# Triangle inversions of two chunks interleaved as four streams, sample state update between their steps

## The chip, the cores and the metric

One core of one Trainium2 chip runs the kernel in a single launch. The metric is device time in microseconds. The kernel before took 1852.71 us (median of three runs, 1852.44 to 1855.36).

## The reference

One inference step of a two-layer decoder with shared weights, for a prompt of 256 tokens and a sample batch of 8 sequences with one token each (264 token columns), all in float32. The first layer is a gated DeltaNet beside a cross-attention, the second a pooling mixer beside a cross-attention with eight experts behind it. The change lies in the DeltaNet alone:

```python
# prompt: chunked delta rule, 8 heads of 128x128
a_mat = I + where(strict, beta * (k k^T) * decay, 0)     # unit lower triangle
w_val, k_cd = solve(a_mat, [v * beta, k * beta * exp(G)])
for each chunk n:
    u = w_val - k_cd @ s
    o = (q * exp(G)) @ s + ((q k^T) * decay) @ u
    s = s * c_decay + k_tail^T @ u
# sample: one token for each of 8 sequences, 64 states of 128x128
s = s * exp(g);  u = b * (v - k @ s);  s = s + k^T u;  o = q @ s
# both: norm over each head, times silu(z), then the output projection
o = o * rsqrt(mean(o*o) + eps) * o_norm * silu(z)
h = x + concat([o, cross_attention]) @ w_out
```

## The kernel before

Everything is transposed: features lie on the 128 partitions, tokens along the free axis. The prompt's 256 tokens are two chunks (`NCH` = 2, the index `c`) of `P` = 128 tokens, with 8 heads (`H`), so that one array over all heads of a chunk is 128x1024 and fills one of the four two-bank PSUM tiles `PP[0..3]` (`bank(b)` is half of one). An ordinary float32 matmul appears as two passes in the trace (8 heads are x16), a transposition as one. Each engine runs its own list in the order in which it is written, and semaphores (`s("...")`) join the lists. There is no scheduler.

The part around the change has these steps:

- Preparation of a chunk. TensorE forms the broadcast cumulative gate (L1512, semaphore `dl_grow`), the two Gram products (L1516, `dl_kk`) and the broadcast beta (L1520, `dl_brow`). VectorE adds the mask (L997, `dl_neg`), ScalarE takes eight exponentials (L660) and one more (L662), VectorE forms `PTb` (L1002), `MTb` (L1004 and L1006), the decayed queries (L1009), the values by token (L1012) and `ktail` (L1014). TensorE transposes values and keys between them (L1527, L1531).
- Inversion of the unit triangle, in seven levels of block doubling (`NLVL` = 7). Level 0 is VectorE's alone (L1023, L1027). Each of the six others is a chain: VectorE masks `MTb` to `MLb` (L1023), TensorE transposes `Ub` (L1542), ScalarE copies it out (`Tb`, L668), TensorE multiplies (L1550), ScalarE copies (`Xb`, L671), TensorE multiplies (L1556), VectorE subtracts from `Ub` (L1032). The eight heads go in two groups of four. Chunk 1 starts when chunk 0 has been finished.
- The chunk's result: `solve` (L1570), copy (L673), output (L1578), state step (L1582), state (L1042, L1046, L1047). Chunk 1 needs the state of chunk 0 (L1564, L1037, L1038).
- The sample part, after both chunks: 64 products of keys and queries with the 64 states (L1593), a short chain on small tiles (L1079 to L1086), then four rounds `r` in which VectorE spreads the updates (`block`, L1093), TensorE forms outer products in four 32-row strips (`outer`, L1609), and VectorE updates 16 states (`new_state`, L360).
- The head norm over all 264 columns: squares (L690), sums (L1616), root (L692), gate (L1098), reciprocal (L1115), each head's row spread to all partitions (L1439), product (L1104). Then the halves for the output projection (L525, L844).
- The output projection `a_out`, 8 chunks of weights with 36 matmuls each (L1357). Large products work on float32r high and low halves: ScalarE forms the high half of the weights (`dense_high`, L334), VectorE the low half (`dense_low`, L340). Weights arrive in two raw slots `draw` at the start of `ring`; two sets of halves `dhi`, `dlo` follow, and their place holds the 64 sample states until these have been stored (POOL's queue, L463).

In the `order` rows below `gen`, `ring`, `ubuf` and `small` are the buffers out of which the arrays are cut; `PP` is PSUM.

## Time and profile before

| | us |
|---|---|
| median of three runs | 1852.71 |
| profiled execution, its own time | 1857.21 |
| its span | 1855.6 |
| PE busy | 1698.1 (92%) |
| DVE busy | 1291.1 (70%) |
| ACT busy | 1070.5 (58%) |
| DMA | 498.81 MB, mean 269 GB/s |

PE is TensorE's matmuls and PEld its weight loads, DVE is VectorE, ACT ScalarE, POOL GpSimd, SPq the DMA queue of SyncE. All times are us from the start of the span. A row of the timeline has the start, the duration from the first start to the last end, the engine, the line, the operation, tile written <- tiles read, the shape, the count, and in brackets the idle time before it and what ended that. A row of busy time by stretch has the stretch, its length, the busy time and count of PE, PEld, DVE, ACT and POOL, PE's granted clock as a share of 2.4 GHz, the share of the DMA engines and GB/s. A row of the chain of waits has start, duration, engine, tile, line and count. A row of DMA issues has the tile and source, the queue, count, size and median us from issue to landing.

### The profile page before, as it was taken

The page shows a single profiled execution, that of the slowest core. Times are in us where ns is not written, and L with a number is a line of the kernel's source. Part 1 is how long each engine was busy: PE and PEld are TensorE (multiplying, and loading weights), DVE is VectorE, ACT ScalarE, POOL GpSimd, SP SyncE. Part 2 cuts the span into 40 slices and gives each one's busy share as a digit, 9 for nine tenths or more (in the row PEclk, how much of TensorE's full clock was granted, in tenths as well). Part 3 has the DMA queues.
Part 4 walks back from the last instruction along what each step waited for, and adds up shares of the span by engine and source line. Part 5 has one row for each costly group of instructions (what it writes and reads, how often), then busy time and mean ns, then how long its engine had stood idle before and what let it go on. Part 6 is the DMA issues. An engine that isn't in the chain of part 4 may idle for free.

```text
span 1855.6 us, 25087 instructions
## 1 busy us (share of the span) xinstructions
PE 1698.1 (92%) x9859; PEld 1455.3 (78%) x9859; DVE 1291.1 (70%) x1160; ACT 1070.5 (58%) x1050; POOL 56.1 (3%) x80
## 2 busy tenths in 40 slices
PE   6999677878999986689999999999999999999993
PEld 6999466748999985587887878878878788787883
DVE  4596334375555455355888888888888888888886
ACT  5565223323443342244777777777777777777774
POOL 0000030000000000002000000000000000000001
PEclk9999779969999999687999999999999999999997
DMA  5555292025454542565999999999999999999993
GB/s 211 186 181 187 91 358 95 1 94 198 151 182 154 185 153 95 208 273 206 379 357 386 354 376 380 353 386 366 359 392 345 387 371 358 392 361 358 385 354 143
DMA packets 74675, 498.81 MB, mean 269 GB/s; under 512 B 8520, under 2 KB 8776, under 8 KB 20848
## 3 DMA queue, kind: packets, MB, share of 16 engines
q1 hardware_dynamic: 65680, 463.33, 65.7%
q0 software_dynamic: 8928, 34.54, 5.0%
q8 instruction: 48, 0.79, 0.2%
q14 instruction: 19, 0.16, 0.0%
HBM read 469.07 MB, written 28.77 MB: 268 GB/s over the span
## 4 chain that ended last, share of the span: by engine, by line
PE 84%; DVE 8%; ACT 4%; DMA 3%; issue 1%; POOL 0%; ACTq 0%; POOLq 0%; SPq 0%; DVEq 0%
PE PP L1357 71%; PE PP L1550 1%; ACT whi L769 1%; PE PP L1759 1%; PE PP L1556 1%; PE PP L1351 1%; DVE wlo L1218 1%; DMA ring<-in_kc 1%; PE PP L1735 1%; DVE ring L360 1%; DVE ring L1023 1%; DMA ring<-in_vc 1%; DVE dlo L340 1%; PE PP L1493 1%; PE PP L1467 0%
## 5 line engine op out<-in xcount | busy, mean ns | idle before, releaser
L1218 DVE TENSOR_TENSOR wlo<-raw,whi 128x2048 fp32r<-128x2048 f32 x339 | 775.1, 2291 | 139.4 <-ACT whi L769 139.1
L769 ACT ACTIVATE whi<-raw 128x2048 fp32r<-128x2048 f32 x339 | 649.3, 1919 | 229.9 <-PE PP L1357 229.8
L1357 PE MATMUL PP<-whi,xsh 128*128 128x512 f32 x896 | 359.3, 401 | 3.6 <-DVE xsl L1266 2.5
L1357 PE MATMUL PP<-wlo,xsh 128*128 128x512 f32 x896 | 354.9, 396 | 0.0
L1357 PE MATMUL PP<-whi,xsl 128*128 128x512 f32 x896 | 354.9, 396 | 0.0
L340 DVE TENSOR_TENSOR dlo<-ring,dhi 128x2048 fp32r<-128x2048 f32 (+2 forms) x86 | 177.9, 2069 | 144.6 <-ACT dhi L334 144.6
L334 ACT ACTIVATE dhi<-ring 128x2048 fp32r<-128x2048 f32 (+2 forms) x86 | 149.0, 1734 | 143.2 <-PE PP L1357 120.1
L1357 PE MATMUL PP<-uh,dhi 128*128 128x264 f32 x736 | 212.4, 289 | 8.9 <-DVE ul L844 8.4
L1357 PE MATMUL PP<-ul,dhi 128*128 128x264 f32 x736 | 210.9, 286 | 0.0
L1357 PE MATMUL PP<-uh,dlo 128*128 128x264 f32 x736 | 210.5, 286 | 0.0
L1357 PEld LDWEIGHTS PP<-whi,xsh 128*128 128x128 f32 x896 | 169.2, 189 | 46.5 <-DVE wlo L1218 5.4
L1357 PEld LDWEIGHTS PP<-whi,xsl 128*128 128x128 f32 x896 | 169.1, 189 | 40.6
L1357 PEld LDWEIGHTS PP<-wlo,xsh 128*128 128x128 f32 x896 | 169.3, 189 | 37.8
L1357 PE MATMUL PP<-whi,hTh 128*128 128x512 f32 x448 | 178.2, 398 | 0.0
L1357 PE MATMUL PP<-whi,hTl 128*128 128x512 f32 x448 | 176.9, 395 | 0.0
L1357 PE MATMUL PP<-wlo,hTh 128*128 128x512 f32 x448 | 176.9, 395 | 0.0
L1357 PEld LDWEIGHTS PP<-uh,dhi 128*128 128x128 f32 x736 | 140.4, 191 | 10.5 <-issue 9.1
L1357 PEld LDWEIGHTS PP<-ul,dhi 128*128 128x128 f32 x736 | 140.7, 191 | 0.0
L1357 PEld LDWEIGHTS PP<-uh,dlo 128*128 128x128 f32 x736 | 140.2, 191 | 0.0
L1357 PEld LDWEIGHTS PP<-whi,hTl 128*128 128x128 f32 x448 | 84.2, 188 | 20.0
L1357 PEld LDWEIGHTS PP<-wlo,hTh 128*128 128x128 f32 x448 | 84.3, 188 | 19.4
L1357 PEld LDWEIGHTS PP<-whi,hTh 128*128 128x128 f32 x448 | 84.3, 188 | 19.3
(374 smaller groups left out, 2011.6 us busy)
## 6 DMA issues: line engine op xcount, KB each, us to landing
raw<-in_w_e SPq DMA_DIRECT2D x339, 1024.0 KB, 4.9
ring<-in_wi SPq DMA_DIRECT2D x22, 1024.0 KB, 4.8
ring<-in_a_in SPq DMA_DIRECT2D x18, 1024.0 KB, 4.8
slot_rows<-ring POOLq DMA_DIRECT2D x25, 512.0 KB, 16.9
ring<-in_wo SPq DMA_DIRECT2D x16, 704.0 KB, 4.1
ring<-in_mkv SPq DMA_DIRECT2D x8, 1024.0 KB, 4.8
ring<-in_kc SPq DMA_DIRECT2D x8, 1024.0 KB, 6.1
ring<-in_vc SPq DMA_DIRECT2D x8, 1024.0 KB, 4.8
```

The lines of the kernel that those rows point to most:

```text
L334: a.activation(halves(n)[0], x, ACT.Copy).then_inc(s("d_hi"), 1)
L340: v.tensor_tensor(low, draw[n % DRAW][:, 0:WIDTH[DENSE[n][0]]], high.bitcast(F32), ALU.subtract)\
L360: ins_ = v.scalar_tensor_tensor(out=sl, in0=sl, scalar=sgb[:, n:n + 1], in1=bank(g)[:, q * P:(q + 1) * P], op0=ALU.mult, op1=ALU.add)
L769: a.activation(whi[c % XSET][:, :], raw_of(c), ACT.Copy).then_inc(s("w_hi"), 1)
L1023: v.tensor_tensor(heads(MLb), heads(MTb), mask, ALU.mult).then_inc(s("dl_ml"), 1)
L1218: v.tensor_tensor(wlo[c % XSET][:, :], raw_of(c), whi[c % XSET][:, :].bitcast(F32), ALU.subtract)\
L1351: mm = pe.matmul(bank(0)[:, 0:n], ones[:, :], sqb[:, k * n:(k + 1) * n], start=(k == 0), stop=(k == KD - 1))
L1357: mm = pe.matmul(out, lhs[l], rhs[r], start=first and i == 0, stop=last and i == 2)
L1493: mm = pe.matmul(bank(3)[32 * x:32 * x + 32, 0:P], p_diag[:, at_:at_ + 32], w[:, col:col + P], start=(b == 0 and m == 0), stop=(b == NS - ...
L1550: mm = pe.matmul(PP[1][:, x * P:(x + 1) * P], MLb[:, x * P:(x + 1) * P], Tb[:, x * P:(x + 1) * P], start=True, stop=True)
L1556: mm = pe.matmul(PP[2][:, x * P:(x + 1) * P], Xb[:, x * P:(x + 1) * P], Ub[:, x * P:(x + 1) * P], start=True, stop=True)
L1735: mm = pe.matmul(PP[1][:, k * C:(k + 1) * C], xtok[0:n, t, k * P:(k + 1) * P], disp[0:n, t, :], start=(t == 0), stop=(t == 2))
```

## The change

Both chunks are prepared first, chunk 1's products being issued between those of chunk 0. Their inversions run level by level together: four streams (`st`; chunk `st // 2`, heads `4 * (st % 2)` to `+ 3`), each in one PSUM bank (0 to 3) in which all three of its products land one after the other. The arrays of chunk 1 have places of their own: in `ubuf`, in the free end of `gen`, and in the two raw weight slots at the start of `ring`; therefore SyncE's loads of the first two `a_out` chunks wait for `dl_r` and for `dl_ds` 2. The sample part uses banks 4 to 7. Its columns are laid out right after the attention, its 64 products are issued ahead of level 1, its small chain stands in level 1, and its four rounds in levels 2 to 5. The head norm is made once for columns 0 to 127 and once for columns 128 to 263 (`parts`), the first while chunk 1's result is being formed. The halves of `cat` are formed in one instruction for attention, one for part 0 and two for part 1. POOL starts its 25 zero-fill DMAs at `state_loaded` and not at `dl_neg`, and stores the sample states before the prompt's state.

The diff, cut to what the prediction speaks of:

```diff
...
-        DTb, MTb, MLb, Xb, PTb, Sb = (cut(ring, arena + 1024 * i, 1024) for i in range(6))
+        DTb = cut(ring, arena, 1024)
+        MTb = [cut(ring, arena + 1024, 1024), cut(ring, 0, 1024)]
+        MLb = [cut(ring, arena + 2048, 1024), DTb]
+        PTb = [cut(ring, arena + 4096, 1024), cut(ring, 2048, 1024)]
...
-        Tb, Ub, vtok, ktail = (cut(gen, SC + 1024 * i, 1024) for i in range(4))
+        Tb = [cut(gen, SC, 1024), cut(ubuf, 1024, 1024)]
+        Ub = [cut(gen, SC + 1024, 1024), cut(ubuf, 0, 1024)]
+        vtok = [cut(gen, SC + 2048, 1024), cut(ring, 1024, 1024)]
+        ktail = [cut(gen, SC + 3072, 1024), cut(ring, 3072, 1024)]
+        Sb = cut(gen, SC + 5840, 1024)
+        Xb = [cut(ring, arena + 3072, 1024), cut(gen, SC + 6864, 1024)]
...
+                if (kind, i) == ("a_out", 0):
+                    sp.wait_ge(s("dl_r"), 1)
+                if (kind, i) == ("a_out", 1):
+                    sp.wait_ge(s("dl_ds"), 2)
...
-            pool.wait_ge(s("dl_neg"), 1)
+            pool.wait_ge(s("state_loaded"), 64)
...
+            for lv in range(1, NLVL):
+                for st in range(4):
+                    a.wait_ge(s("dl_tt"), 4 * (lv - 1) + st + 1)
+                    a.activation(half(Tb[st // 2], st % 2), bank(st), ACT.Copy).then_inc(s("dl_t"), 1)
+                for st in range(4):
+                    a.wait_ge(s("dl_xx"), 4 * (lv - 1) + st + 1)
+                    a.activation(half(Xb[st // 2], st % 2), bank(st), ACT.Copy).then_inc(s("dl_x"), 1)
...
+            inverted(0)
+            a.wait_ge(s("dl_um"), 4 * NLVL)
+            a.wait_ge(s("att_cat"), 2)
+            a.activation(cat_h[:, H:H + XH, :], cat[:, H:H + XH, :], ACT.Copy).then_inc(s("m_hi"), 1)
+            a.wait_ge(s("dl_o"), 1)
+            a.activation(cat[:, 0:H, parts[0]], PP[3][:, :].rearrange("p (m c) -> p m c", m=H), ACT.Copy).then_inc(s("dl_cat"), 1)
+            a.wait_ge(s("dl_cat"), 1)
+            squares(0)
+            head_root(0)
+            inverted(1)
+            a.wait_ge(s("on_done"), 1)
+            a.activation(cat_h[:, 0:H, parts[0]], cat[:, 0:H, parts[0]], ACT.Copy).then_inc(s("m_hi"), 1)
+            a.wait_ge(s("state_stored0"), 32)
+            dense_high(a, AT["a_out", 0])
+            a.wait_ge(s("dl_o"), 2)
+            a.activation(cat[:, 0:H, SEQ - P:SEQ], PP[2][:, :].rearrange("p (m c) -> p m c", m=H), ACT.Copy).then_inc(s("dl_cat"), 1)
             a.wait_ge(s("dl_cat"), NCH)
             a.wait_ge(s("sd_cat"), 1)
-            for x in range(H):
-                a.activation(sq[:, x * T:(x + 1) * T], cat[:, x, :], ACT.Square).then_inc(s("on_sq"), 1)
-            a.wait_ge(s("on_mm"), 1)
-            a.activation(rt[:, 0:T], bank(4)[:, 0:T], ACT.Sqrt, bias=epsc[:, 0:1], scale=1.0 / P).then_inc(s("head_rt"), 1)
-
-            a.wait_ge(s("att_cat"), 2)
-            high(cath[0], cat, T, range(H, H + XH), lambda k: None)
-            a.wait_ge(s("state_stored0"), 32)
-            dense_high(a, AT["a_out", 0])
-            high(cath[0], cat, T, range(H), lambda k: a.wait_ge(s("on_done"), k + 1))
+            squares(1)
+            head_root(1)
+            for i in range(2):
+                a.wait_ge(s("on_done"), 2 + i)
+                a.activation(cat_h[:, 4 * i:4 * i + 4, parts[1]], cat[:, 4 * i:4 * i + 4, parts[1]], ACT.Copy).then_inc(s("m_hi"), 1)
...
+                if c:
+                    v.wait_ge(s("dl_dt"), H)
+                    v.wait_ge(s("dl_mt"), 2)
+                    first_level(0)
...
+            for lv in range(1, NLVL):
+                if lv == 1:
+                    sample_rows()
+                if lv == 2:
+                    block(0)
+                if 2 <= lv < 5:
+                    block(lv - 1)
+                if 2 <= lv < 6:
+                    new_state(v, lv - 2)
+                if lv + 1 < NLVL:
+                    level_mask(lv + 1, 0)
+                for st in range(4):
+                    v.wait_ge(s("dl_du"), 4 * (lv - 1) + st + 1)
+                    u_half = Ub[st // 2][:, st % 2 * 512:(st % 2 + 1) * 512]
+                    v.tensor_tensor(u_half, u_half, bank(st), ALU.subtract).then_inc(s("dl_um"), 1)
+                if lv + 1 < NLVL:
+                    level_mask(lv + 1, 1)
...
+            v.wait_ge(s("dl_ds"), 1)
+            v.tensor_copy(Sb, PP[2][:, :]).then_inc(s("S_done"), 1)
+            cat_low(H, H + XH, slice(0, T))
+            v.wait_ge(s("dl_ks"), 1)
+            link(v.tensor_tensor(heads(Xb[1]), heads(PP[0][:, :]), per_head(1, cbeG), ALU.mult))
+            v.tensor_tensor(Xb[1], vtok[1], Xb[1], ALU.subtract).then_inc(s("dl_r"), 1)
+            gated(0)
+            head_inverse(0)
+            v.wait_ge(s("on_mm"), 2)
+            v.tensor_tensor(cat[:, 0:H, parts[0]], cat[:, 0:H, parts[0]], heads(PP[3][:, :]), ALU.mult).then_inc(s("on_done"), 1)
+            cat_low(0, H, parts[0])
             dense_low(v, AT["a_out", 0])
+            gated(1)
...
+            v.wait_ge(s("dl_ds"), NCH)
+            v.wait_ge(s("dl_o"), NCH)
+            link(v.tensor_tensor(heads(Sb), heads(Sb), per_head(1, ceGl), ALU.mult))
+            v.tensor_tensor(Sb, Sb, PP[0][:, :], ALU.add).then_inc(s("S_done"), 1)
+            dense_low(v, AT["a_out", 1])
...
+            def four(st):
+                return range(4 * (st % 2), 4 * (st % 2) + 4)
+
+            for lv in range(1, NLVL):
+                n0 = 4 * (lv - 1)
+                for st in range(4):
+                    c = st // 2
+                    if lv == 1:
+                        pe.wait_ge(s("dl_kt") if c == 0 else s("dl_mt"), 1 if c == 0 else 3)
+                    pe.wait_ge(s("dl_um"), 4 * (lv - 1) + st + 1)
+                    for x in four(st):
+                        mm = pe.transpose(PP[c][:, head(x)], Ub[c][:, head(x)], ident)
+                    mm.then_inc(s("dl_tt"), 1)
+                if lv == 1:
+                    pe.wait_ge(s("sd_row"), 1)
+                    pe.transpose(bank(7)[:, 0:P], kqrow, ident).then_inc(s("sd_mm"), 1)
+                if 2 <= lv < 6:
+                    outer(lv - 2)
+                for st in range(4):
+                    c = st // 2
+                    pe.wait_ge(s("dl_ml"), 2 * lv + c + 1)
+                    pe.wait_ge(s("dl_t"), n0 + st + 1)
+                    for x in four(st):
+                        mm = pe.matmul(PP[c][:, head(x)], MLb[c][:, head(x)], Tb[c][:, head(x)], start=True, stop=True)
+                    mm.then_inc(s("dl_xx"), 1)
+                if lv == 1:
+                    pe.wait_ge(s("sd_u"), 1)
+                    pe.wait_ge(s("sd_row"), 2)
+                    pe.transpose(bank(6)[:, 0:P], upad, ident).then_inc(s("sd_rows"), 1)
+                for st in range(4):
+                    c = st // 2
+                    pe.wait_ge(s("dl_x"), n0 + st + 1)
+                    for x in four(st):
+                        mm = pe.matmul(PP[c][:, head(x)], Xb[c][:, head(x)], Ub[c][:, head(x)], start=True, stop=True)
+                    mm.then_inc(s("dl_du"), 1)
...
+            solve(0, vtok[0])
+            pe.wait_ge(s("state_new"), 14)
+            state_step(0, PP[2])
+            pe.wait_ge(s("state_new"), 16)
+            result(0, PP[3])
+            pe.wait_ge(s("S_done"), 1)
             for x in range(H):
-                j, r = x % 4, x // 4
-                pe.wait_ge(s("on_sq"), x + 1)
-                mm = pe.matmul(bank(4)[32 * j:32 * j + 32, 0:T], pick[:, 31 - r:63 - r], sq[:, x * T:(x + 1) * T],
-                               start=(r == 0), stop=(r == H // 4 - 1))
+                mm = pe.matmul(PP[0][:, head(x)], act[:, 8 + x, cols(1)], Sb[:, head(x)], start=True, stop=True)
+            mm.then_inc(s("dl_ks"), 1)
+            pe.wait_ge(s("dl_cat"), 1)
+            head_sums(0, bank(6), 0, P)
+            pe.wait_ge(s("dl_r"), 1)
+            solve(1, Xb[1])
+            pe.wait_ge(s("head_inv"), 2)
+            for x in range(H):
+                col = 32 * (x % 4) + x // 4
+                mm = pe.matmul(PP[3][:, head(x)], ident[:, col:col + 1].to_broadcast([P, P]), rs[:, 0:P], start=True, stop=True)
             mm.then_inc(s("on_mm"), 1)
-            outer(1)
-            pe.wait_ge(s("head_inv"), 2)
-            for x in range(4):
-                row_to_all(bank(4 + x)[:, 0:T], rs, x).then_inc(s("on_mm"), 1)
-            outer(2)
-            for x in range(4, H):
-                pe.wait_ge(s("on_done"), x - 3)
-                row_to_all(bank(4 + x % 4)[:, 0:T], rs, x).then_inc(s("on_mm"), 1)
-            outer(3)
-            pe.wait_ge(s("state_new"), 16)
-            pe.wait_ge(s("on_done"), H)
+            pe.wait_ge(s("dl_qd"), 2)
+            result(1, PP[2])
+            state_step(1, PP[0])
+            head_sums(1, bank(2), P, T - P)
+            pe.wait_ge(s("head_inv"), 3)
+            pe.wait_ge(s("dl_cat"), 2)
+            pe.wait_ge(s("on_done"), 1)
...
```

TensorE's list at the end of chunk 0's inversion, before the change; L1542, L1550 and L1556 are the transposition and the two products of a level, L1570 to L1582 the chunk's result, L1512 to L1531 the preparation of chunk 1:

```order
L1542 MATMUL PP<-consts,gen 128x128 x8
L1550 MATMUL PP<-gen,ring 128x128 x8
L1556 MATMUL PP<-gen,ring 128x128 x8
L1570 MATMUL PP<-gen 128x128 x8
L1578 MATMUL PP<-ring,gen 128x128 x8
L1582 MATMUL PP<-gen 128x128 x8
L1512 MATMUL PP<-consts,small 128x128 x8
L1516 MATMUL PP<-ring 128x128 x16
L1520 MATMUL PP<-consts,small 128x128 x8
L1527 MATMUL PP<-consts,ring 128x128 x8
L1531 MATMUL PP<-consts,ring 128x128 x8
```

And one of the levels 2 to 5 with the change; `gen` holds `Ub` of chunk 0 and `ubuf` that of chunk 1, L1649 is the transposition, L1635 the sample's outer products, L1661 and L1671 the two products:

```order
L1649 MATMUL PP<-consts,gen 128x128 x8
L1649 MATMUL PP<-consts,ubuf 128x128 x8
L1635 MATMUL PP<-gen 128x512 x4
L1661 MATMUL PP<-gen,ring 128x128 x8
L1661 MATMUL PP<-ubuf,ring 128x128 x8
L1671 MATMUL PP<-gen,ring 128x128 x8
L1671 MATMUL PP<-ubuf,gen 128x128 x8
```

A level now holds both chunks and one round of outer products; results and preparations have left the place between the levels.

VectorE's list of the sample rounds and the head norm before the change; L1093 is `block`, L360 `new_state`, L1098, L1115 and L1104 the head norm:

```order
L1093 TENSOR_TENSOR gen<-gen 128x512 x2
L1098 SCALAR_TENSOR_TENSOR gen<-ring,gains,gen 128x264 x4
L360 SCALAR_TENSOR_TENSOR ring<-ring,small,PP 128x128 x16
L1093 TENSOR_TENSOR gen<-gen 128x512
L1098 SCALAR_TENSOR_TENSOR gen<-ring,gains,gen 128x264 x4
L1115 RECIPROCAL gen<-gen 128x264
L360 SCALAR_TENSOR_TENSOR ring<-ring,small,PP 128x128 x16
L1093 TENSOR_TENSOR gen<-gen 128x512
L1104 TENSOR_TENSOR gen<-gen,PP 128x264 x4
L360 SCALAR_TENSOR_TENSOR ring<-ring,small,PP 128x128 x32
```

And from the mask of chunk 0 in level 2 on with the change; L1066 is the mask, L1141 the subtraction of chunk 0 (`gen`) and of chunk 1 (`ubuf`), L1124 `block`, L368 `new_state`:

```order
L1066 TENSOR_TENSOR ring<-ring,consts 128x1024
L1141 TENSOR_TENSOR gen<-gen,PP 128x512 x2
L1141 TENSOR_TENSOR ubuf<-ubuf,PP 128x512 x2
L1066 TENSOR_TENSOR ring<-ring,consts 128x1024
L1124 TENSOR_TENSOR gen<-gen 128x512
L368 SCALAR_TENSOR_TENSOR ring<-ring,small,PP 128x128 x16
```

Each round of 16 state updates stands between two masks of the inversion.

SyncE's list with the change, where the loads of the output projection's weights follow those of the sample states:

```order
L389 DMA ring<-in_state 128x2048 [waits ain_mm]
L389 DMA ring<-in_state 128x2048 x3
L398 DMA ring<-in_a_out 128x1536 [waits cache_mm,dl_r]
L398 DMA ring<-in_a_out 128x1536 [waits cache_mm,dl_ds]
L398 DMA ring<-in_a_out 128x1536 [waits d_lo] x6
```

Before, the first two of the eight `in_a_out` loads waited for `cache_mm` alone.

## Rows read from the trace of the kernel before

**Rows 1.** The page's chain that ended last, share of the span by engine:

```profile
PE 84%; DVE 8%; ACT 4%; DMA 3%; issue 1%; POOL 0%; ACTq 0%; POOLq 0%; SPq 0%; DVEq 0%
```

**Rows 2.** Busy time by stretch: preparation, result, levels, result, sample, projection, experts:

```profile
243.40:260.70 17.30, 12.22 (x80) 11.78 (x81) 10.36 (x10) 3.35 (x9) 11.55 (x19) 0.80 1.01 404
299.00:322.60 23.60, 15.25 (x129) 14.46 (x129) 11.56 (x12) 5.40 (x11) 0.00 (x0) 0.97 0.00 1
322.60:360.70 38.10, 32.81 (x240) 29.63 (x240) 16.06 (x19) 14.33 (x24) 0.00 (x0) 0.93 0.00 1
360.70:380.30 19.60, 11.36 (x80) 10.73 (x80) 6.64 (x21) 2.05 (x2) 0.55 (x1) 0.88 0.03 13
380.30:418.20 37.90, 28.09 (x197) 15.82 (x198) 30.32 (x95) 10.60 (x26) 2.13 (x4) 0.55 0.28 116
418.20:456.00 37.80, 37.67 (x288) 37.48 (x288) 21.26 (x27) 14.21 (x15) 0.00 (x0) 0.93 0.54 185
850.00:1150.00 300.00, 298.67 (x1313) 241.35 (x1314) 255.34 (x157) 222.15 (x147) 11.80 (x12) 0.99 0.94 365
```

**Rows 3.** Timeline of one inversion level of chunk 0:

```profile
292.17 0.66 PE L1542 MATMUL PP<-consts,gen 128*128 128x128 f32 x4
292.86 0.60 ACT L668 ACTIVATE gen<-PP 128x512 f32<-128x512 f32 x1 [1.79 <-PE PP L1542]
...
293.11 1.23 DVE L1023 TENSOR_TENSOR ring<-ring,consts 128x1024 f32<-128x1024 f32 x1
...
294.39 2.05 PE L1550 MATMUL PP<-gen,ring 128*128 128x128 f32 x16 [0.67 <-DVE ring L1023]
...
296.28 2.01 PE L1556 MATMUL PP<-gen,ring 128*128 128x128 f32 x16
...
297.43 0.69 DVE L1032 TENSOR_TENSOR gen<-gen,PP 128x512 f32<-128x512 f32 x1 [3.10 <-PE PP L1556]
298.33 0.69 DVE L1032 TENSOR_TENSOR gen<-gen,PP 128x512 f32<-128x512 f32 x1 [0.21 <-PE PP L1556]
```

**Rows 4.** Timeline, the first level of chunk 1:

```profile
324.41 3.73 PE L1550 MATMUL PP<-gen,ring 128*128 128x128 f32 x16
```

**Rows 5.** Timeline of chunk 1's preparation:

```profile
309.34 3.74 PE L1516 MATMUL PP<-ring 128*128 128x128 f32 x32
...
310.87 2.44 ACT L660 ACTIVATE ring<-ring,small 128x128 f32<-128x128 f32 x8 [5.52 <-DVE ring L997]
...
313.22 1.00 ACT L662 ACTIVATE ring<-PP 128x1024 f32<-128x1024 f32 x1
...
316.99 1.23 DVE L1009 TENSOR_TENSOR ring<-ring 128x1024 f32<-128x1024 f32 x1
318.14 1.22 DVE L1012 TENSOR_TENSOR gen<-PP,small 128x1024 f32<-128x1024 f32 x1
```

**Rows 6.** Timeline of the sample part:

```profile
380.36 6.42 PE L1593 MATMUL PP<-ring,gen 128*32 128x128 f32 x128 [4.52 <-DVE gen L1074]
...
390.21 2.09 PE L1609 MATMUL PP<-gen 32*128 32x512 f32 x8 [1.19 <-DVE gen L1093]
...
392.29 4.22 DVE L360 SCALAR_TENSOR_TENSOR ring<-ring,small,PP 128x128 f32<-128x128 f32 x16
...
398.65 1.80 DVE L1115 RECIPROCAL gen<-gen 128x264 f32<-128x264 f32 x1
```

**Rows 7.** Timeline, the halves of the first output-projection weights:

```profile
408.94 1.48 ACT L334 ACTIVATE dhi<-ring 128x1536 fp32r<-128x1536 f32 x1 [12.93 <-DMA out_state<-ring]
...
415.98 1.75 DVE L340 TENSOR_TENSOR dlo<-ring,dhi 128x1536 fp32r<-128x1536 f32 x1
```

**Rows 8.** Chain of waits, the output projection:

```profile
418.23 37.68 PE PP L1357 x288
```

**Rows 9.** DMA issues of the output projection's weights and the prompt's state:

```profile
ring<-in_a_out SPq DMA_DIRECT2D x8, 768.0 KB, 4.3
...
out_S<-ring POOLq DMA_DIRECT2D x1, 512.0 KB, 2.9
```

More of the change, by code:

```diff
@@ L227, in build @@
         kqrow = cut(gen, DS + 704, 128)
-        kpad = cut(gen, DS + 1728, 128)
-        upad = cut(gen, DS + 1856, 128)
-        own16 = cut(gen, DS + 1984, 16)
-        assert 4096 + 2000 <= SCN
+        own16 = cut(gen, DS + 1728, 16)
+        kpad, upad = (cut(ring, arena + 6400 + 128 * i, 128) for i in range(2))
+        assert 4096 + 1744 <= 5840 and 6400 + 256 <= CT * PRE
         urow = cut(gen, DS + 576, 128)
@@ new lines, in inverted, with squares @@
+            def inverted(c):
+                for g in range(2):
+                    a.wait_ge(s("dl_uu"), 2 * c + g + 1)
+                    a.activation(half(Tb[c], g), bank(2 * c + g), ACT.Copy).then_inc(s("dl_u"), 1)
+            cat_h = cath[0].rearrange("p (k t) -> p k t", t=T)
+            parts = (slice(0, P), slice(P, T))
+            def squares(c):
+                sqv = sq.rearrange("p (k t) -> p k t", t=T)
+                a.activation(sqv[:, :, parts[c]], cat[:, 0:H, parts[c]], ACT.Square).then_inc(s("on_sq"), 1)
@@ L1124, in _ @@
-            dense_low(v, AT["a_out", 0])
-            v.wait_ge(s("S_stored"), 16)
-            for k in range(H, H + XH):
-                low(catl[0], cath[0], cat, T, k)
-            for k in range(H):
-                low(catl[0], cath[0], cat, T, k)
-            dense_low(v, AT["a_out", 1])
-            def residual(name, chunks):
+            for lv in range(1, NLVL):
[15 more added lines that the diff above has]
+                    level_mask(lv + 1, 1)
@@ L1581, in _ @@
-                for x in range(H):
-                    mm = pe.matmul(PP[3][:, x * P:(x + 1) * P], ktail[:, x * P:(x + 1) * P], uu[:, x * P:(x + 1) * P],
-                                   start=True, stop=True)
-                mm.then_inc(s("dl_ds"), 1)
-            pe.wait_ge(s("dl_cat"), NCH)
-            pe.wait_ge(s("S_done"), NCH)
+            pe.wait_ge(s("att_cat"), 2)
+            grow(0, PP[0])
+            gram(0, 0, PP[1])
+            gram(0, 8, PP[2])
+            brow(0, PP[3])
@@ new lines, in solve, with state_step @@
+            def solve(c, R):
+                for g in range(2):
+                    pe.wait_ge(s("dl_um"), 4 * (NLVL - 1) + 2 * c + g + 1)
+                    for x in four(g):
+                        mm = pe.matmul(PP[c][:, head(x)], Ub[c][:, head(x)], R[:, head(x)], start=True, stop=True)
+                    mm.then_inc(s("dl_uu"), 1)
+            def state_step(c, out):
+                for x in range(H):
+                    if x % 4 == 0:
+                        pe.wait_ge(s("dl_u"), 2 * c + x // 4 + 1)
+                    mm = pe.matmul(out[:, head(x)], ktail[c][:, head(x)], Tb[c][:, head(x)], start=True, stop=True)
+                mm.then_inc(s("dl_ds"), 1)
@@ L1632, in _ @@
+            pe.wait_ge(s("dl_cat"), 2)
+            pe.wait_ge(s("on_done"), 1)
+            for x in range(H):
+                at_, r = 32 * (x % 4), x // 4
+                mm = pe.matmul(bank(4 + x % 4)[:, r * (T - P):(r + 1) * (T - P)],
+                               ident[at_:at_ + 32, at_ + r:at_ + r + 1].to_broadcast([32, P]),
+                               rs[at_:at_ + 32, P:T], start=True, stop=True)
+            mm.then_inc(s("on_mm"), 1)
             order = [(k, k) for k in (*range(H, H + XH), *range(H))]
```

366 lines of the change are left out of this document (168 added, 198 removed).

## The prediction

> **What bounds the kernel now.** I read the page's chain of waits first: 84% of it is TensorE [rows 1], so only what shortens TensorE's path, or a stretch in which it waits, can show. Then busy time by stretch [rows 2]. The projection and the experts keep TensorE busy to over 99%, and the change does not touch them. Between the end of the attention (243.4) and the projection (418.2) that is not so: TensorE is busy for 12.2 of 17.3 us in the first preparation, 15.3 of 23.6 between the chunks, 11.4 of 19.6 behind chunk 1, and in the sample part for 28.1 of 37.9, there at a granted clock of 0.55, with VectorE busy for 30.3. Even the levels hold it for only 32.8 of 38.1 us. Third, the timeline of one level [rows 3] shows why: mask (1.23), product, product, subtraction run one behind the other. From the mask's start at 293.11, through the second product at 296.28, to the last subtraction at 298.33 plus 0.69, it is 5.9 us, 6.0 with the handover, in which TensorE has 40 passes. Twelve such levels are 72 us.
>
> **The change, on the time axis of the profile before.** Nothing moves before 243.4. The sample's column layout (2 us of small VectorE work) now stands there, beside TensorE's first products, and costs nothing: it used to follow chunk 1. Its cover is the 3.9 us between 243.4 and the first mask; without it, it would cost its 2 us.
>
> *Preparation of both chunks.* VectorE sets it. An operation of 128x1024 takes 1.23 us, and 1.15 from start to start where nothing is awaited (316.99 to 318.14) [rows 5]. Chunk 0 ends at about 258.4, as before. Chunk 1: gate mask 1.15 (259.6); the eight exponentials 2.44 on ScalarE (262.1), beside which VectorE makes level 0 of chunk 0; a ninth of 1.00 and TensorE's broadcast of beta, 16 passes at half of the 3.74 for 32, take until 265.1 [rows 5]; then the last product and three more, 1.23 + 3 x 1.15 = 4.7, to 269.8. Then TensorE makes the sample's 64 products, 6.42 [rows 6], and three small ones, 0.5: level 1 begins at 276.8. Beside them VectorE makes level 0 of chunk 1 and two masks, 1.2 + 1.3 + 2.3 = 4.8 us, which is covered.
>
> *Levels.* Both chunks make 80 passes in a level. 16 take 1.89 from start to start (294.39 to 296.28) [rows 3], so a level is 9.45 us if TensorE never waits. It need not: one stream's way through a level is 0.66 + 0.60 + 1.1 + 0.60 + 1.1 + 0.69 = 4.8 us, half a level, so three other streams cover it. ScalarE has eight copies of 0.60, 4.8 us. VectorE has two masks and four subtractions, 2 x 1.23 + 4 x 0.69 = 5.2 us. In levels 2 to 5 it also has 16 state updates, 4.22 [rows 6], and a `block` of the subtraction's shape, 0.69: 10.1 us. Outer products join TensorE there. Before, eight of their passes took 2.09 at half clock [rows 6]; at full clock they lie between half of that and all of it. I take 1.9, near the row, and keep 1.05 as the other end. So levels 2 to 5 are 11.35 on TensorE against 10.1 on VectorE, and TensorE leads. Level 1 has two small transpositions (0.4), level 2 waits for the first `block` (0.75). Sum: 9.85 + 12.1 + 3 x 11.35 + 9.45 = 65.45, from 276.8 to 342.2. Where VectorE leads instead, the four levels are 10.4 with handovers, so cheap outer products save at most 3.8.
>
> The Trainium skill (TensorEngine Tiling (Array Packing), Key Properties) speaks against this placing: a change of the tiling mode drains TensorE. Outer products of 32 rows now stand four times between full-array products, eight changes. The drain in this trace is what a run outlasts the start of the next: 2.05 against 1.89, 0.16 us [rows 3]. Eight of them are 1.3 us; by the rule the sum would be 1.3 later, inside my range; I leave it out, since nothing here shows a change of mode apart.
>
> *Behind the levels.* Chunk 0's solve, state step, output, and the keys times state are four runs of 16 passes, 7.6 (349.8, 350.0 with the tail). VectorE's two operations on the right side, 2 x 1.23, to 352.5. Solve of chunk 1, 1.9, to 354.4; at the same time VectorE's gate (1.25) and reciprocal (1.80 for 264 columns [rows 6], so 0.9 for 128), to 354.65. Spreading 1.9 (356.55), output of chunk 1 3.8 (360.3), state step 1.9 behind it (362.2). ScalarE has finished high halves of `cat` and weights by then (359.0 + 1.48 = 360.5 [rows 7]), copies the output (1.0), squares it (1.05): 362.6. Sums 0.8 (16 of the 128 passes in 6.42), root 0.4, reciprocal 0.95, spreading 1.1, two products 1.4, high and low half 0.65 each: 368.9. TensorE has meanwhile made the projection's attention part, begins with the heads at 368.9 and has 24 passes at 37.68 / 288 = 0.131 [rows 8], to 372.05. That rate contains an opening at half clock, as before. Then the second set of weights: VectorE makes its low half behind both halves of `cat` (369.6) and the state update (2 x 1.23), 1.75 [rows 7], ready at 373.85. Seven tiles of 36 passes, 33.0: end at 406.9.
>
> *DMAs.* The first two weight loads lose their early start. The first goes out at 352.5 and takes 4.3 [rows 9], 356.8, before ScalarE asks for it at 359.0: covered by 2.2 us. The second goes out at 362.3 and is there at 366.6, ScalarE comes to it at 368.8: covered by 2.2. The sample's stores end inside the levels (the last update is made near 328), and the 12.93 us that ScalarE waited for them go [rows 7]. The prompt's state is stored from 372.1 and takes 2.9 [rows 9]; VectorE waits for that (375.0) before the first residual addition and the third low half, which it then has at 377.2, while TensorE wants it at 378.6.
>
> *Sum.* Before, the stretch from 243.4 to the projection's end at 455.9 is 212.5 us; after it is 163.5. That is 49 us less. The profiled execution took 1857.2 (span 1855.6), so its like would take 1808; the median of the runs is 4.5 us below it, 1852.7, and the forecast for the median is 1804. What is late next is VectorE and ScalarE in turns between 350 and 374. All of the experts' stage is relative to what precedes it and moves along.
>
> **Rivals.**
>
> *Half clock behind the levels.* After its pause before 324.4, TensorE took 3.73 for 16 passes instead of 2.05 [rows 4, 3], and the sample part with its short runs had a clock of 0.55 [rows 2]. The new tail has pauses of 1 to 3 us too (350.0 to 352.5, 363.4 to 365, 366.1 to 368.9). If the clock falls at the first, solve, spreading, output and two small runs double: 1.9 + 1.9 + 3.8 + 1.4 = 9 us, giving 1813. For it: the pauses. Against: runs of 4 to 8 us stand between them. The Trainium skill (TensorE: Matmul & The Clock Gate, HAM oscillation) says that waits between bursts put the engine back to the half clock each time; if so here, it is this rival's time, and the sample part's 0.55 agrees.
>
> *VectorE becomes the bound of levels 2 to 5.* If its 4.22 + 0.69 of sample work does not fit beside the products, because it is queued between two masks and TensorE waits for the subtractions behind it, each of the four levels grows by up to 4.9 us: 19.6, giving 1824. For it: 10.1 of 11.35 us is little room. Against: the state updates wait only for outer products that stand early in the level, and the subtractions come last anyway.
>
> *Half clock in all levels, and slower than before.* The place is the six joint levels. If the mixture of 32-row and full-array passes with waits on four streams keeps the clock low, as in the sample part [rows 2], 80 passes take 18.9 instead of 9.45, 57 us more in all, giving 1861, 8 slower than now. It decides from 49 / 9.45 = 5.2 levels at half clock on. Against it: with pauses in every level, the chunk-1 stretch of before had a mean of 0.93, low only at its opening, and at 99% busy the experts have 0.99 [rows 2].
>
> *Better than the sum.* Outer products at 1.05, the sample's products faster at full clock than their 6.42, part of the weights' rate at full clock: 8 us, 1796.
>
> *The change doesn't do what it says.* The order shows that it does; waits which tie streams to each other would make a level as long as before, 12 us for both chunks, 15 us more, 1819.
>
> **Chances.** The sum, within 1799 to 1809: 0.58. Half clock behind the levels 0.17, better than the sum 0.10, VectorE as the bound 0.05, tied streams 0.03, the slower rival 0.03, and 0.04 for what I don't see. The range runs from 1793 (below the better case by its unknowns) to 1817 (above the half-clock case), leaving out 0.15 or so. About 0.2%, 3.7 us, is what a measurement of this kernel tells from no change: faster by more 0.95, within it 0.02, slower by more 0.03.
>
> **What would show it.** Right: levels 1 and 6 of 9.5 to 10 us and levels 2 to 5 of 10.4 to 11.5, TensorE over 95% busy there at a clock near 1; the first transposition of level 1 near 276.8; no wait of ScalarE for the state's stores; the projection's last matmul near 407. Wrong: subtractions that start more than 1 us behind their products (VectorE), passes of 0.23 us behind 350 (clock), TensorE waiting for halves of weights at the second or third tile (the delayed loads).

## Result and profile after

The changed kernel takes 1798.84 us (median of four runs), the kernel before 1852.62 beside it: a ratio of 0.9706, 95% interval 0.9682 to 0.9730. The forecast was 1804, with a range of 1793 to 1817. The four runs lie at 1795.7, 1796.2, 1801.5 and 1801.8; the profiled execution took 1801.81.

The head of the page of after, its TensorE line, the granted clock in 40 slices, and its chain by engine:

```profile
span 1800.2 us, 25098 instructions
...
PE 1674.6 (93%) x9891; PEld 1444.9 (80%) x9891; DVE 1287.6 (72%) x1142; ACT 1067.9 (59%) x1039; POOL 57.1 (3%) x81
...
PEclk9999869999999995969999999999999999999997
...
PE 86%; DVE 5%; ACT 4%; DMA 3%; issue 1%; POOL 0%; ACTq 0%; POOLq 0%; SPq 0%; DVEq 0%
```

Against 1698.1 us before, TensorE is busy for 23.5 us less, while its instructions are nearly the same. Part of that is clock: from the attention's end to the projection's, the granted clock was 0.85 before and is 0.95 now. Another part is not: a short run is counted as busy until its last pass has ended, so that the 40 passes of one of the old levels were busy for 5.1 us at a clock of 1.00, while 40 passes of a joint level take 4.45. The rest of the gain is idle time that went. Busy time by stretch of after (columns as in [rows 2]): preparation of both chunks with the sample's products, the six levels, the tail up to the projection's first heads, the projection, the experts.

```profile
243.30:275.20 31.90, 26.93 (x292) 26.10 (x292) 24.35 (x37) 6.96 (x19) 18.47 (x25) 0.85 0.87 296
275.20:334.80 59.60, 58.83 (x518) 55.05 (x517) 47.66 (x109) 27.20 (x51) 2.15 (x4) 1.00 0.49 175
334.80:362.60 27.80, 23.38 (x205) 21.97 (x203) 16.34 (x16) 13.37 (x17) 0.00 (x0) 0.88 0.24 86
362.60:398.70 36.10, 34.12 (x276) 33.69 (x276) 20.36 (x19) 14.21 (x15) 1.49 (x2) 1.00 0.52 182
850.00:1150.00 300.00, 299.66 (x1336) 242.10 (x1335) 259.29 (x143) 223.97 (x147) 2.17 (x4) 1.00 0.98 368
```

Where TensorE was busy for 32.8 of 38.1 us of one chunk's levels [rows 2], it is busy for 58.8 of 59.6 in those of both, at a clock of 1.00. The projection ends at 398.2 (its last pass begins at 397.95) where it ended at 455.9: 57.7 us of the stage are gone, and 49 were forecast. The experts have not changed.

The chain of waits of after through one joint level (start, duration, engine, tile, line, passes). L1649 are the transpositions, L1635 the outer products, L1661 and L1671 the two products:

```profile
295.47 1.75 PE PP L1649 x16
297.22 1.07 PE PP L1635 x8
298.29 3.77 PE PP L1661 x32
302.06 3.57 PE PP L1671 x32
305.63 1.75 PE PP L1649 x16
```

It holds TensorE alone: 10.16 us for both chunks, against 6.0 for one [rows 3]. The last level, without outer products, takes 8.9 (325.95 to 334.84).

### The profile page after: what moved, and what is told of

It reads as the page before. It is cut to its first block, busy times and chain, and to the rows that moved or that the text cites. A ratio compares the mean times of both kernels' runs of the same rounds, so it can differ in the third digit from the quotient of the medians.

```text
span 1800.2 us, 25098 instructions
## 1 busy us (share of the span) xinstructions
PE 1674.6 (93%) x9891; PEld 1444.9 (80%) x9891; DVE 1287.6 (72%) x1142; ACT 1067.9 (59%) x1039; POOL 57.1 (3%) x81
## 4 chain that ended last, share of the span: by engine, by line
PE 86%; DVE 5%; ACT 4%; DMA 3%; issue 1%; POOL 0%; ACTq 0%; POOLq 0%; SPq 0%; DVEq 0%
PE PP L1418 73%; ACT whi L809 1%; PE PP L1870 1%; PE PP L1661 1%; PE PP L1412 1%; PE PP L1671 1%; DMA ring<-in_vc 1%; DVE wlo L1279 1%; DMA ring<-in_kc 1%; PE PP L1846 1%; DVE dlo L348 1%; PE PP L1528 1%; ACT dhi L342 1%; PE PP L1554 1%; ACT L809 0%
```

## Experiments

The time is not the best measure of an edit here, since runs of one kernel differ by up to 7 us. The profile has a better one: the start of the sums of squares behind the projection (L1412; L1351 before), where the stage is over. From there to the end of the span is 1399.2 us before (from 456.42), 1401.1 after (from 399.12), and between 1397.9 and 1401.4 in all twelve other profiles. So each edit is read from the "end of the stage", and its median is set beside it. That measure has noise of its own, ahead of the levels: in the kernels whose preparation is the same, level 1 starts between 271.45 and 277.67, in part because TensorE's short runs there come at full or at half clock (the sample's 64 products took 3.70 in some profiles, 5.37 in others). Where an edit stands behind that point, the distance from there to the end of the stage says more.

### The changed kernel again

> The changed kernel again, for a closer ratio and a second profile: its four runs lay in two pairs, 1795.7 and 1796.2 against 1801.5 and 1801.8. Theory: the pairs come from where the half clock falls, so the mean granted clock goes with the time (0.955 against 0.950), and the stretch from 243 to the projection's end is the same within 1 us in both profiles. Rival: the joint levels themselves vary from run to run.

Five runs: median 1796.03 (1794.63 to 1799.07), ratio 0.9689 (0.9676 to 0.9703). In the nine runs so far the mean granted clock goes with the time, as expected: 0.950 to 0.953 in the three above 1799 us, 0.955 to 0.957 in the other six. The joint levels take 59.6 again. The stage ends at 398.72, 0.4 earlier; the span is 3.1 shorter. The chains of after and then of this profile show where most of it arises, in the next layer's attention:

```profile
674.72 5.97 PE PP L1528 x16
...
692.14 4.94 DMA ring<-in_vc
699.12 7.12 DMA ring<-in_vc
```

```profile
673.47 3.73 PE PP L1528 x16
...
695.54 6.46 DMA ring<-in_vc
```

The same 16 passes took 5.97 at a granted clock of 0.62 and 3.73 at one of 1.00 (2.2 us), and one wait for a cached V more in the chain. No edit here touches these; they set what two single runs can tell.

### Sample rounds behind the levels, then chunk by chunk, then the mask last

Three kernels, each built on the one before it. The first takes the outer products and state updates out of the levels and puts them between the last level and chunk 0's solve:

```diff
-                if 2 <= lv < 6:
-                    outer(lv - 2)
...
+            for r in range(4):
+                outer(r)
             solve(0, vtok[0])
```

> The changed kernel with the sample's four rounds (block, outer products, state updates) behind the six joint levels and ahead of chunk 0's solve. In the changed kernel the levels run from 275.2 to 334.8, 59.6 us. Theory (TensorE leads every level, the rounds ride beside it): the levels shrink only by their outer products (4 x 1.07) and the wait of level 2 (0.8), to 54.5 us, and the rounds, bare, cost VectorE's 4 x 4.2 + 1.3 = 18 us, of which TensorE waits about 15: 10 us slower than the changed kernel, about 1809, at 0.976 of before. Rival (VectorE leads the levels with a round, so a round costs nearly its own length there too): the levels shrink by 15 or more, and the time stays within 3 us of the changed kernel.

The second makes all levels of chunk 0 and then all of chunk 1, with two streams each; masks still stand ahead of the subtractions:

```diff
-            for lv in range(1, NLVL):
-                for st in range(4):
+            for k in range(2 * (NLVL - 1)):
+                c, lv = k // (NLVL - 1), k % (NLVL - 1) + 1
+                for g in range(2):
```

> As e1, and the levels chunk by chunk: two streams at a time, all six levels of chunk 0, then those of chunk 1, with the mask of the next level still formed ahead of the subtractions. Theory (only four streams keep TensorE busy; with two it waits for the copies and subtractions as in the kernel before): a level is about 6.0 us, 72 in all, 17 us slower than e1. Rival (what made the levels short is that the mask left the chain between subtraction and product): a stream's way is 4.8 us and TensorE's work for two streams 4.5, so a level is 5.0 to 5.3 us, 60 to 64 in all, 6 to 9 us slower than e1.

The third puts each mask behind the subtractions, as the kernel before had it:

```diff
-                if lv + 1 < NLVL:
-                    level_mask(lv + 1, c)
                 for g in range(2):
...
+                if lv + 1 < NLVL:
+                    v.wait_ge(s("dl_um"), 4 + 2 * k + 2)
+                    level_mask(lv + 1, c)
```

> As e2, with the mask of the next level behind the subtractions and awaited by the product, as in the kernel before. Both theories: 6.0 us a level, 72 in all, 17 us slower than e1; by the theory of the four streams no slower than e2, by the rival of the mask 8 to 12 us slower than e2. If it is well under 72, then the place of the mask is not what sets the 6.0 us of the kernel before.

| kernel | median | ratio, interval | levels (first start) | end of the stage |
|---|---|---|---|---|
| changed | 1798.84 | 0.9706 (0.9682 to 0.9730) | 59.6 (275.20) | 399.12 |
| rounds behind | 1811.19 | 0.9780 (0.9763 to 0.9796) | 53.8 (274.62) | 411.66 |
| by chunk | 1821.40 | 0.9836 (0.9820 to 0.9852) | 64.1 (273.80) | 421.06 |
| mask last | 1828.20 | 0.9874 (0.9857 to 0.9890) | 69.7 (271.45) | 426.65 |

Windows of the first kernel, its levels and then its rounds:

```profile
274.60:328.40 53.80, 53.76 (x484) 53.57 (x482) 29.81 (x41) 27.21 (x51) 0.00 (x0) 1.00 0.34 113
329.00:346.70 17.70, 15.67 (x33) 5.92 (x33) 17.09 (x62) 0.00 (x0) 1.62 (x3) 0.64 0.33 138
```

Without the rounds a level is 8.9 us of nothing but TensorE. Behind the levels they are VectorE's (17.1 of 17.7 us busy), and TensorE's clock falls to 0.64. From the last product of the levels to chunk 0's solve it is 18.3 us (328.4 to 346.7). So the rounds cost 18.3 alone and 5.8 inside: 12.5 us. That is the theory of the expectation, with 2.5 us more than it put down; the rival, in which VectorE leads the levels, is out.

The chain of the second kernel through a level of one chunk:

```profile
311.03 0.70 DVE ubuf L1137
311.78 0.66 PE PP L1648 x4
312.50 2.02 PE PP L1657 x16
314.52 1.86 PE PP L1666 x16
316.40 0.70 DVE ubuf L1137
```

5.37 us for 40 passes, which alone would be 4.45: the last subtraction and the handovers now stand in the chain. Two streams are not enough to cover what follows a product; four are. The levels are 10.3 us longer for it (64.1 against 53.8). Of the two expectations, the theory (6.0 us a level, 72 in all) was wrong, and the rival (5.0 to 5.3, 60 to 64) nearly right. In the third kernel the mask joins the chain:

```profile
312.26 1.24 DVE ring L1067
313.54 2.05 PE PP L1658 x16
315.59 1.86 PE PP L1667 x16
317.47 0.70 DVE ubuf L1135
318.19 1.24 DVE ring L1067
```

5.93 us, nearly the 6.0 of [rows 3]; the mask's place is worth 5.7 us of the levels (69.7 against 64.1), less than the 8 to 12 of the expectation. The stage ends 5.6 later too, but that is chance: level 1 began 2.35 earlier here, and behind the levels as much was lost again, most of it with chunk 1's solve, 3.64 at half clock against 2.05. So what the prediction put down as one thing, a TensorE that never waits, has two causes, the streams and the masks' place. The three steps make 27.5 of the 57.3 us, to within the 2 or 3 us by which the clock shifts such stages; the other 29.8 lie in what is common to all of them: one preparation for both chunks, the sample's small operations moved out of the way, the tail. They were not separated further, but for the next edit.

### Head norm behind chunk 1

The changed kernel with both halves of the norm behind chunk 1's output:

```diff
-            a.wait_ge(s("dl_cat"), 1)
-            squares(0)
-            head_root(0)
             inverted(1)
...
+            squares(0)
             squares(1)
+            head_root(0)
             head_root(1)
```

> The changed kernel with the whole head norm behind chunk 1's output, both column parts one right behind the other. Theory (part 0 of the norm is hidden beside chunk 1's solve and output): squares 1.1, sums 0.7, gate 1.3, reciprocal 0.95, spreading 1.8, product 1.2 and the halves 2.3 of part 0 come onto the path behind 354, some of it beside part 1: 5 to 8 us slower than the changed kernel. Rival (the path there is TensorE's own passes and the weights' halves, and the norm has room): under 2 us.

1808.92 (1805.09 to 1810.51), ratio 0.9763 (0.9747 to 0.9779). The stage ends at 407.40, 8.3 later; 1.3 of that arose ahead of the levels, so 7 are left for the norm's two parts; in them is a spreading of 16 passes at half clock, 3.34 (the changed kernel has 1.95 for its own). The expectation was 5 to 8; the medians are 10 to 13 apart, more than the stage explains.

### Does VectorE or TensorE set levels 2 to 5?

Three kernels, with one run each: a quarter of the state updates (three quarters of the sample's new state are left out), one more VectorE operation of 128x512 in each of levels 2 to 5, and the outer products made twice:

```diff
-                for q in range(4):
+                for q in range(1):
```

> The changed kernel with only 4 of the 16 state updates of each round, which leaves three quarters of the sample's new state out: VectorE is relieved of 3.1 us in each of levels 2 to 5. In the changed kernel such a level takes 10.16 us. Theory (TensorE leads): 10.1 to 10.2 again. Rival (VectorE leads, TensorE's work fits in less): down to 9.9 or less.

```diff
                     new_state(v, lv - 2)
+                    block(lv - 2, extra=True)
```

> The changed kernel with one more 128x512 operation of VectorE (0.65 us) in each of levels 2 to 5. VectorE's work there is 4.2 + 0.65 + 2 x 1.15 + 4 x 0.65 = 9.75 of 10.16 us. Theory (TensorE leads, but by 0.4 us only): the level grows by 0.2 to 0.4 us, to 10.4 to 10.6. Rival (ample room): 10.16. Rival (VectorE leads already): 10.8.

```diff
+                    pe.matmul(bank(4 + g), krow[32 * g:32 * g + 32, :], ublk[r % 2][32 * g:32 * g + 32, :], start=True, stop=True)
+                for g in range(4):
```

> The changed kernel with each round's outer products formed twice: TensorE has 8 more passes of 32 rows, about 1.07 us, in levels 2 to 5. Theory (TensorE leads): each level grows by 0.9 to 1.1 us. Rival (VectorE leads): by under 0.7.

The six levels, 59.6 in the changed kernel, take 59.6 with a quarter of the updates (277.67 to 337.32), 59.6 with more VectorE work (274.97 to 334.61) and 63.1 with twice the outer products (275.34 to 338.42). Times: 1802.79, 1801.60, 1803.64. TensorE sets the levels. I had expected a little growth from the added VectorE operation; there is none, so at least its 0.69 us fits into each level.

TensorE around the outer products, from the timeline of the kernel that makes them twice:

```profile
308.20 1.04 PE L1651 MATMUL PP<-consts,ubuf 128*128 128x128 f32 x8
...
309.17 1.14 PE L1635 MATMUL PP<-gen 32*128 32x512 f32 x8
...
310.13 1.04 PE L1637 MATMUL PP<-gen 32*128 32x512 f32 x8
...
311.10 2.05 PE L1663 MATMUL PP<-gen,ring 128*128 128x128 f32 x16
```

Eight more passes with no change of tiling cost 0.86 us a level (11.02 against 10.16), 0.108 each. The first eight cost 1.26 (10.16 against 8.90). The 0.40 between them goes with the two changes between full-array and 32-row passes: four times 0.40 is 1.6 us. The Trainium skill (TensorEngine Tiling (Array Packing), Key Properties) says that a change of mode drains the engine; the prediction put that at 1.3 by the tail of a run and left it out. The 1.6 agree with the rule, though a drain is not seen apart from whatever else happens at those borders.

### Three edits where the changed kernel still waits, and all together

Four rows of the chain of after stand for four places where it could be shorter:

```profile
262.82 3.67 PE PP L1582 x16
...
271.18 3.70 PE PP L1621 x128
...
344.69 3.68 PE PP L1679 x16
...
365.59 1.68 DVE dlo L348
```

beta's broadcast of chunk 1 at half clock, with VectorE waiting; the sample's 64 products ahead of level 1; chunk 1's solve at half clock; the low half of the second weights, made behind the state update. First, that low half goes ahead of the update:

```diff
+            dense_low(v, AT["a_out", 1])
             v.wait_ge(s("dl_ds"), NCH)
...
-            dense_low(v, AT["a_out", 1])
-            v.wait_ge(s("S_stored"), 16)
```

> The changed kernel with VectorE's low half of the second projection weights ahead of the update of the prompt's state, and the wait for that state's store moved from before the first residual addition to before the pooling input is written. In the changed kernel TensorE waits 1.50 us for this half at its second tile (365.8 to 367.3). Theory (the order on VectorE is what holds it): the wait goes to 0.1 or less, the projection ends 1.2 to 1.5 us earlier. Rival (the late load of the second weights holds it): the wait stays over 1 us.

Second, in the preparation, beta's broadcast waits for less (another PSUM tile), chunk 0's first mask and transpositions go ahead of the sample's:

```diff
-            pe.wait_ge(s("dl_neg"), 2)
-            pe.wait_ge(s("dl_eg"), 2)
-            brow(1, PP[2])
+            pe.wait_ge(s("dl_kt"), 1)
+            brow(1, PP[0])
```

> The changed kernel with chunk 1's broadcast of beta in the PSUM tile of chunk 0's keys, so that it need not wait for the ninth exponential, and the sample's 64 products in a bank of their own, ahead of chunk 1's last VectorE operations. In the changed kernel VectorE waits 2.35 us for the broadcast (formed at half clock, 3.65 us, after a pause of TensorE of 2.2), and the 64 products stand 4.0 us ahead of level 1. Theory (these two waits set the preparation): the first product of level 1 starts at 273 and not at 277.05, and the time falls by 3.5 to 4.5 us. Rival (VectorE's list alone sets it): it falls by 2.4 at most.

Third, matmuls without use fill two of TensorE's pauses in the tail:

```diff
+            for x in range(6):
+                pe.matmul(bank(3)[:, 0:P], ident, tri, start=True, stop=True)
             pe.wait_ge(s("dl_r"), 1)
             solve(1, Xb[1])
```

> The changed kernel with 12 and 14 idle passes of TensorE into a free bank in its two pauses behind the levels (343.2 to 344.7 and 356.7 to 358.4). In the changed kernel chunk 1's solve runs at half clock, 3.68 us instead of 1.9, and so do the first ten projection passes. Theory (the pauses bring the half clock, and short work in them prevents it): the solve takes 1.9, the passes 0.12 each, and the time falls by 2 to 3 us. Rival (the clock fell for what went before, the sum over it being low anyway): the solve still takes over 3 us, no gain.

Last, all three:

> The three edits of e8, e9 and e10 together. Theory (they stand in different places of one chain): the gains add, 7 to 9 us below the changed kernel, about 1788, at 0.965 of before. Rival (each moves the wait to another engine): 3 to 5 us.

| kernel | median (runs) | ratio, interval | end of the stage | from level 1's first product to there |
|---|---|---|---|---|
| changed | 1798.84 (1795.72 to 1801.81) | 0.9706 (0.9682 to 0.9730) | 399.12 | 122.1 |
| changed, again | 1796.03 (1794.63 to 1799.07) | 0.9689 (0.9676 to 0.9703) | 398.72 | 121.5 |
| low half first | 1798.46 (1796.39 to 1799.05) | 0.9693 (0.9672 to 0.9713) | 396.15 | 118.8 |
| preparation | 1795.43 (1793.78 to 1799.35) | 0.9684 (0.9661 to 0.9706) | 393.56 | 120.3 |
| filled pauses | 1797.87 (1797.02 to 1799.18) | 0.9692 (0.9672 to 0.9712) | 397.61 | 119.9 |
| all three | 1791.01 (1789.15 to 1796.14) | 0.9664 (0.9643 to 0.9685) | 389.81 | 118.2 |

Alone, none can be told from the changed kernel by its time. By the end of the stage they are 2.6 to 3.0, 5.2 to 5.6 and 1.1 to 1.5 us ahead, but not all of that is the edit. In all of them chunk 1's solve took 2.05 and not 3.68 or 3.49, and the first two edits touch nothing between the levels and that solve. Its row in the changed kernel and in that with the low half first:

```profile
344.69 3.68 PE L1679 MATMUL PP<-gen,ubuf 128*128 128x128 f32 x16 [1.42 <-DVE gen L1168]
```

```profile
344.99 2.05 PE L1679 MATMUL PP<-gen,ubuf 128*128 128x128 f32 x16 [1.43 <-DVE gen L1168]
```

What is left of each edit:

- Low half first: from the first pass with heads to the end of the stage it is 35.0 (from 361.14), against 36.1 to 36.5 in seven profiles in which TensorE waits 1.5 for that half. So its place is worth 1.1 to 1.5 us, as expected; the rest is the solve.
- Preparation: from chunk 1's exponentials to the first product of level 1 it is 14.1 us here and with all three edits, against 17.6 to 19.0 in the other kernels with joint levels. The first product starts at 273.27; 273 was expected. The rest, again, is the solve.
- Filled pauses: the 1.5 to 2.1 us behind level 1's first product are hardly more than what the preparation kernel has there without any filling (1.2 to 1.8).

Together the three are 8.9 to 9.3 ahead, near the sum and at the upper end of the 7 to 9 expected, with the lowest time of all: 5 us below the better of the two medians of the changed kernel. Of this, 1.7 us arose ahead of the three edits: chunk 1's exponentials began at 257.56, against 259.31 in the changed kernel. (The intervals of the ratios still touch, so 5 us is what the medians say, and 9 what the profiles say.) The chain of that version, the projection in one piece:

```profile
354.61 0.73 DVE catl L1160
355.39 33.91 PE PP L1418 x276
```

and its tail, at full clock where after had 0.88:

```profile
329.40:355.40 26.00, 23.62 (x231) 22.02 (x230) 16.37 (x16) 13.39 (x17) 0.00 (x0) 1.00 0.25 92
```

What the filling itself gives isn't settled, since chunk 1's solve ran at full clock in four kernels without it (rounds behind, by chunk, low half first, preparation). That in its own kernel no pass of the tail was slow (granted clock 1.00) is what was seen.

## Why the prediction was right

The mechanism is the one forecast, and the time, 1798.84 and then 1796.03, lies in the range. It lies just below the 1799 to 1809 of "the sum", though: the stage lost 57.7 us and not 49, and the terms below say where.

*What bounds it, and what leads in the levels: right.* TensorE leads; shown by adding and taking away VectorE work (nothing) and TensorE work (all of it). The rival with VectorE as the bound is out, as are tied streams and half clock in the levels (1.00 throughout).

*Preparation: right in its end, by two errors that cancel.* The first transposition of level 1 starts at 275.20, forecast 276.8. The timeline of after:

```profile
262.82 3.65 PE L1582 MATMUL PP<-consts,small 128*128 128x128 f32 x16 [2.22 <-ACT gen L678]
...
266.51 1.22 DVE L1092 TENSOR_TENSOR ring<-ring,PP 128x1024 f32<-128x1024 f32 x1 [2.35 <-PE PP L1582]
...
271.18 3.70 PE L1621 MATMUL PP<-ring,gen 128*32 128x128 f32 x128 [2.31 <-DVE ring L1098]
```

Beta's broadcast took 3.65 for the 1.9 of the sum: half clock, behind a pause of 2.22. The sample's products took 3.70 for 6.42: that row [rows 6] was itself at half clock, which its stretch's clock of 0.55 said [rows 2]. I named this as an error to come only in the rival "better than the sum". That the two cancel is luck, and so is the size of each: in the second profile of the changed kernel the broadcast took 2.50 and the products 5.37, and level 1 still started at 275.39.

*Levels: mis-sized.* 65.45 forecast, 59.6 measured. 80 passes take 8.9, not 9.45: I took 16 passes as 1.89 from start to start, which held 0.1 us of something that the interleaved streams don't show; 32 passes take 3.57, so 16 take 1.79. That is 3.3 over six levels. The outer products I took at 1.9, near a row at half clock, with 1.05 as the other end; eight of them take 1.07 in the chain and 1.26 with what they do to their neighbours: 2.6 over four. The wait for the first `block` was right (0.77 for 0.75). So the levels were shorter than the bounds named as the sign of being right (9.5 to 10, and 10.4 to 11.5): 8.9 to 9.1, and 10.16.

*Tail: right in sum, 32.5 against 31.7 from the last level to the second tile.* Solve of chunk 1 at half clock (1.8) was a part of the rival "half clock behind the levels", as were the projection's first nine passes, 0.22 apart (0.9); so was the spreading of the norm's second part, 1.29 where it takes 0.74 with the low half first (0.5). The other spreading, the output and the sums were not slow. So about 3.2 of that rival's 9 us came, and how much of it comes is luck: with the low half first, whose order is the same up to there, the solve ran at full clock and the projection's first passes did not. What held the second tile was, as forecast, the low half behind the state update:

```profile
365.51 1.75 DVE L348 TENSOR_TENSOR dlo<-ring,dhi 128x1536 fp32r<-128x1536 f32 x1
...
367.32 0.39 PE L1418 MATMUL PP<-cath,dhi 128*128 128x264 f32 x1 [1.50 <-DVE dlo L348]
```

It came at 367.3, 6.6 earlier than the sum had it: 5.9 from the levels and 1.6 from their start, less 0.9 in the tail.

*Projection: 30.9 for seven tiles, 33.0 forecast.* The rate of 0.131 [rows 8] held its slow opening, which the new one has in the attention part instead; at full clock a pass is 0.123.

*DMAs: right.* ScalarE's 12.93 us for the sample's stores [rows 7] are gone, and neither of the two delayed loads is waited for. In its place in the chain stands a later weight load (`in_wi`, 5.96 us at 388.50) as a releaser, beside the projection; TensorE goes from 367.32 to 398.2 with no pause.

*Sum.* 163.5 forecast for the stage, 154.9 measured. The nearest case was "better than the sum" with its 1796 and 8 us: its three terms came, wholly or in part (outer products near the low end, 2.6; the sample's products, 2.7; the weights' passes, 2.1). The other 3.3, the faster passes of the levels, it didn't have. Half clock took back 1.8 at beta's broadcast and 3.2 in the tail, and most of the latter was made up for elsewhere in the tail, which came out 0.9 longer. By the stage alone the forecast would have been 1795.4. The first median lies 3.4 above that and the second 0.6, while their profiles' stages differ by 0.4, so that difference lies outside the stage. The "slower" rival had nothing: its price was worked out for a clock that never fell in the levels.

## What to carry to other kernels

Where a chain of small steps alternates between engines, count streams: one stream's way round (4.8 us here) must be less than the others' work on the engine that should lead (6.7), and two streams of this kind fell short where four did not. Price an operation by a row at the clock that its new place will have: outer products from a stretch with a clock of 0.55 were priced at about twice what they took where the engine is kept busy. An operation that nobody waits for yet (mask, low half of weights) stands in an in-order queue all the same: its place was worth 5.7 and 1.1 to 1.5 us here. And before a gain in a profile is put down to an edit, find the place where it arises: a solve that the edit did not touch was 1.4 to 1.6 us faster in two of the kernels here.

## What was not expected of the hardware

- Half clock behind short pauses depends on the run. Chunk 1's solve comes behind a pause of about 1.4 us. Among five profiles whose TensorE list is the same up to there, its 16 passes took 3.68, 3.49, 3.68 and 3.68 in four and 2.05 in the fifth (low half first). Beta's broadcast, 3.65 in after behind a pause of 2.22, took 2.50 behind 3.08 and 2.02 behind 2.28 in two others. The Trainium skill (TensorE: Matmul & The Clock Gate, HAM oscillation) tells of a kernel in which longer waits between bursts put the engine back to half clock every time. The runs here show it behind a wait of 1.42 us, and only some of the time.
- 32-row outer products of 512 columns go at 0.108 us a pass, as fast as full-array passes of 128 columns (0.1116), and each pair of mode changes goes with 0.4 us.
- Runs of this kernel on one core differ by up to 7 us (1794.63 to 1801.81). In the two profiles most of the difference arose from clock and DMA waits in the next layer's attention, which no edit touches. So an edit of 3 us is seen in the profile's times before it is seen in a median of five, but only if it is read at the place where it arises.
